# Shifting two operand pairs by 64 bytes in SBUF: block sums against gate and up weights, turned probabilities against values

## The reference

```
def swiglu(x, w_gate, w_up, w_down):
    return (jax.nn.silu(x @ w_gate) * (x @ w_up)) @ w_down
...
    for i in range(DEPTH):
        h = rms_norm(x, ffn1_norm[i])
        x = x + 0.5 * swiglu(h, ffn1_w_gate[i], ffn1_w_up[i], ffn1_w_down[i])
        ...  # the mixer: x = x + even_mixer(...) or odd_mixer(...)
        h = rms_norm(x, ffn2_norm[i])
        x = x + 0.5 * swiglu(h, ffn2_w_gate[i], ffn2_w_up[i], ffn2_w_down[i])
```

## Time and profile before

| | us |
|---|---|
| three runs | 1920.60, 1921.14 (median), 1924.37 |
| the profiled execution, first to last instruction | 1922.5 |
| PE busy in it | 1887.3 |
| DVE busy | 1462.5 |
| ACT busy | 1020.9 |
| POOL busy | 193.0 |

### The profile page before, as it was taken

How to read it: one execution, slowest core, us unless ns; L and a number is a source line. 1 busy time by engine, 2 the same in 40 slices (tenths; PEclk the granted TensorE clock), 3 DMA queues, 4 the chain that set the end, 5 groups by cost and what they waited for, 6 DMA issues and landing times.

```text
span 1922.5 us, 31441 instructions
## 1 busy us (share of the span) xinstructions
PE 1887.3 (98%) x11902; PEld 1674.8 (87%) x11902; DVE 1462.5 (76%) x2330; ACT 1020.9 (53%) x1640; POOL 193.0 (10%) x251
## 2 busy tenths in 40 slices
PE   7999999999999999999999999999999999999999
PEld 6899799888878899898889989887778779898997
DVE  8878487667779778597887949756988878687684
ACT  7546154477776455264644626454455766364451
POOL 1311010000001111010110101011111001011010
PEclk9999999999999999999999999999999999999999
DMA  7666862321126655462466646166765376566441
GB/s 240 169 171 182 131 188 61 110 77 57 65 102 173 170 151 152 149 175 97 136 167 165 166 132 181 50 152 161 171 148 133 85 202 171 157 168 168 133 115 66
DMA packets 94662, 271.18 MB, mean 141 GB/s; under 512 B 10568, under 2 KB 10824, under 8 KB 94512
## 3 DMA queue, kind: packets, MB, share of 16 engines
q1 hardware_dynamic: 63456, 201.22, 31.7%
q0 software_dynamic: 29232, 64.50, 19.4%
q10 hardware_dynamic: 1824, 3.44, 1.0%
HBM read 223.07 MB, written 2.28 MB: 117 GB/s over the span
## 4 chain that ended last, share of the span: by engine, by line
PE 85%; DVE 8%; ACT 3%; issue 2%; DMA 1%; ACTq 0%; DVEq 0%
PE ps_unit L797 12%; PE ps_unit L798 12%; PE ps_unit L799 12%; PE ps_y L861 6%; PE ps_y L863 6%; PE ps_y L862 6%; PE ps_s L861 4%; PE ps_s L863 4%; PE ps_s L862 4%; PE ps_t L861 4%; PE ps_t L863 3%; PE ps_t L862 3%; PE ps_s L797 1%; PE ps_s L798 1%; PE ps_s L799 1%
## 5 line engine op out<-in xcount | busy, mean ns | idle before, releaser
L1398 ACT ACTIVATE gw_hi<-gu 128x512 fp32r<-128x512 f32 (+1 forms) x400 | 318.9, 799 | 151.0 <-PE ps_s L863 67.5
L1932 DVE TENSOR_TENSOR gw_lo<-gu,gw_hi 128x512 fp32r<-128x512 f32 (+1 forms) x400 | 354.8, 901 | 49.0 <-ACT gw_hi L1398 36.7
L797 PE MATMUL ps_unit<-a_hi,w_hi 128*128 128x512 f32 x892 | 352.8, 395 | 9.2 <-DVE w_lo L1860 6.5
L798 PE MATMUL ps_unit<-a_lo,w_hi 128*128 128x512 f32 x892 | 349.1, 391 | 0.0
L799 PE MATMUL ps_unit<-a_hi,w_lo 128*128 128x512 f32 x845 | 330.1, 391 | 0.0
L1333 ACT ACTIVATE w_hi<-raw 128x1024 fp32r<-128x1024 f32 (+1 forms) x125 | 125.2, 1003 | 314.0 <-PE ps_unit L799 296.3
L797 PEld LDWEIGHTS ps_unit<-a_hi,w_hi 128*128 128x128 f32 x892 | 168.4, 189 | 48.8 <-DVE w_lo L1860 9.4
L2065 DVE TENSOR_TENSOR t<-ps_unit,half 128x512 f32<-128x512 f32 x96 | 66.4, 691 | 172.4 <-PE ps_unit L799 171.8
L798 PEld LDWEIGHTS ps_unit<-a_lo,w_hi 128*128 128x128 f32 x892 | 168.4, 189 | 33.2
L799 PEld LDWEIGHTS ps_unit<-a_hi,w_lo 128*128 128x128 f32 x845 | 159.5, 189 | 34.1
L861 PE MATMUL ps_y<-xu_hi,gw_hi 128*128 128x256 f32 x640 | 180.3, 282 | 0.3 <-ACT sqb L1402 0.3
(11 more groups left out here) (322 smaller groups left out, 4666.9 us busy)
## 6 DMA issues: line engine op xcount, KB each, us to landing
gu<-gu_stream_dram SPq DMA_DIRECT2D x176, 512.0 KB, 5.2
raw<-w_stream_dram SPq DMA_DIRECT2D x136, 512.0 KB, 3.3
gu<-gu_stream_dram SPq DMA_DIRECT2D x80, 256.0 KB, 3.0
gu<-gu_stream_dram POOLq DMA_DIRECT2D x80, 256.0 KB, 4.5
gu<-gu POOLq DMA_DIRECT2D x80, 256.0 KB, 3.3
w_lo<-raw POOLq DMA_DIRECT2D x28, 512.0 KB, 5.1
raw<-w_stream_dram SPq DMA_DIRECT2D x32, 384.0 KB, 3.5
w_lo_3rd<-raw POOLq DMA_DIRECT2D x15, 512.0 KB, 5.2
```

The costliest lines, as they stand in the source:

```text
L797: pe.matmul(ps, lhs_hi, rhs_hi, start=first, stop=False)
L798: pe.matmul(ps, lhs_hi, rhs_lo, start=False, stop=False)
L1398: act.activation(gw_hi[:, w, :], src, ACT.Copy).then_inc(gw_hi_done, 1)
L1932: dve.tensor_tensor(gw_lo[:, w, :], src, gw_hi[:, w, :].bitcast(F32), ALU.subtract).then_inc(gw_lo_done, 1)
```

## The change

Three gaps of 64 bytes are put into the layout. One moves xu_hi and xu_lo from 64 to 0 modulo 128 (gw stays at 64); one moves pt_hi and pt_lo in the same way (v stays at 64); the third moves what follows pt by another 64, so that all of these tiles have moved by 128 and keep their place modulo 128. No instruction is added, removed or moved on any engine; only addresses differ.

```
+
+HALF_LINE = 64
+
...
         gw_lo = sb("gw_lo", [P, 7, PIECE], F32R)
+        top[0] += HALF_LINE
         xu_hi = sb("xu_hi", [P, PAIRS, 3 * TH], F32R)
         xu_lo = sb("xu_lo", [P, PAIRS, 3 * TH], F32R)
...
         probs = sb("probs", [P, 2, T])
+        top[0] += HALF_LINE
         pt_hi = sb("pt_hi", [P, 14, P], F32R)
         pt_lo = sb("pt_lo", [P, 14, P], F32R)

+        top[0] += HALF_LINE
         shared = top[0]
```

## The result

The changed kernel takes 1929.41 us (median of five runs, 1927.55 to 1930.11) where the kernel before, run beside it, takes 1921.14 us (1920.54 to 1924.37). The ratio is 1.0036 with a 95% interval of 1.0026 to 1.0047: it is slower, by 5.0 to 9.0 us. The time lies above the predicted range.

What follows compares the result with a forecast made beforehand. The prediction took PE, busy 98% of the span, as the bound. Its terms -3.6 + 7.3 - 0.6 = +3.1 us on the median 1921.1 gave 1924.2 us, stated as 1923.5 us, range 1900 to 1927 us.

Steps and rivals of the forecast that it cites:

- PE sets the time, and its pace is what counts: Whole kernel: PE busy 98% of the span, so longer or shorter matmuls of the long streams are paid almost in full.
- "If xu takes the place of xs", group 1, -3.6 us: Four groups of 324 matmuls: xu also at 113.3 ns, 0.9 us less each, 3.6 us less in all.
- Groups 2 and 3, +7.3 us: Eight groups of 660 matmuls: all keep the slow 117.8 ns, 0.9 us more each, 7.3 us more in all.
- pt and v, -0.6 us: 192 pt matmuls of 256 columns: from 118 towards 113.3 ns, 0.6 us less taken, bounds 0 and 1.3 us less.
- The waits of PE, 0: Groups 2 and 3: one early and one late wait might let the pace become fast; nothing taken for either.
- the 0.7 us that the prediction took off for a freed group: Groups 2 and 3: a wait freeing one now and then takes about a microsecond off, 1924.2 to 1923.5 us.
- The prediction's 1.4 us between the profiled execution and the median: Whole kernel before: profiled execution put 1.4 us over the median of three runs, so the forecast counts from the median.
- the slower rival: Group 1: waits for DVE bring the slow pace, 0.5 us more each; 1930 us; chance 0.07, including a worse new place.
- The fast pace throughout: Groups 1 to 3: all at 113.3 ns, the slow pace kicked out or ending itself; -19.8 us, 1901 us; chance 0.28.
- The rule of the Trainium skill that the prediction weighed: PE: streamed operand and weights read through independent ports, so addresses would not matter; 1921 us; chance 0.06.

## Why the prediction was wrong, step by step

- **PE sets the time, and its pace is what counts.** Right. The difference lies in the 256-column streams, 6.1 us by their bounds. The waits in which the profiles also differ, at 204.95 us and the one of the earlier trace rows, are taken up above and below; neither follows the place of xu alone.
- **"If xu takes the place of xs", group 1, -3.6 us.** This is the step that failed. It took a place to be what the distance leaves modulo 128. By +64 xu came to a new place with a pace of its own, 117.8 ns instead of 113.3, and group 1 won 4 x 0.28 = 1.1 us: 2.5 us less than the term. The mechanism of the term was right for the place meant: at +192 group 1 is 36.73 us, 0.96 less than before. The prediction did have the doubt (+64 against -64 modulo 256), but used it as a condition of a rival and left it out of its own sum.
- **Groups 2 and 3, +7.3 us.** Right: 8 x 0.90 = 7.2 us. The kick that xu gave was gone and the slow pace lasted for all 660 matmuls. It came about by another way than the one assumed: xu does not share the slow pace of xs, it runs at 117.8 ns in group 1 too, beside a fast xs. That the two paces are the same number is luck for this term. At +192 the way is the assumed one: xu runs at 117.8 ns in groups 2 and 3 and at 113.3 in group 1.
- **pt and v, -0.6 us.** Nothing; the kernel with this part alone is at 0.9998 (0.9989 to 1.0007). In the changed kernel nine pt matmuls of 256 columns take 439.42 - 438.36 = 1.06 us, 118 ns each, as six did before:

```profile
438.36 0.28 PE L803 MATMUL ps_y<-pt_hi,v_hi 128*128 128x256 f32 x1
...
439.42 0.22 PE L803 MATMUL ps_y<-pt_hi,v_hi 128*128 128x128 f32 x1
```

- **The waits of PE, 0.** Right for the profile of after, where the wait of the earlier trace rows is missing and no group was freed or lost by it. Elsewhere it is longer than before's 0.25 us: 1.72 us with xu moved by 64, 1.42 by 128, 2.12 by 192, and 0.51 in the second profile of before. These are microseconds that the sum has no term for; what sets their length stays open.
- **What carries it out of the range.** With the step that failed set right, and the 0.6 us of pt taken out, the sum becomes 1921.1 + 7.2 - 1.1 = 1927.2 us, at the end of the stated range; the 0.7 us that the prediction took off for a freed group had no counterpart. The measured median is 2.2 us higher. The baseline may hold most of that: the five runs of before beside the changed kernel have a median of 1921.1 us, the larger sets 1922.0 to 1922.8 us, and 1922.7 + 7.2 - 1.1 = 1928.8 us. That is argued and not shown, and the wait above is another candidate. (The prediction's 1.4 us between the profiled execution and the median compares a span with a device time; like with like it is 1924.37 - 1921.14 = 3.2 us. The sum does not use it.)
- **The rivals.** The time came out close to that of the slower rival, 1930 us, but its mechanism did not take place: in the changed kernel PE has no wait in group 1 of the first block, with DVE busy for 36.15 of 38.20 us there (the windows: PE, PEld, DVE, ACT, POOL):

```profile
38.00:76.20 38.20, 38.20 (x324) 37.21 (x323) 36.15 (x53) 25.87 (x45) 6.19 (x7) 1.00 0.77 206
```

- The fast pace throughout did not come, since xu at +64 does not kick. It is there to be had: xu at +192 with one extra matmul ahead of each group 2 and 3 gives 1905 us, where that rival said 1901. The rule of the Trainium skill that the prediction weighed (page "TensorE: Matmul & The Clock Gate", section "Step-by-step: what each phase is for", two independent read ports) would, read as the prediction read it, have left the kernels that differ in addresses alone equal. The runs disagree with that reading: addresses alone give 113.3, 117.8, 119 or 120 ns for xu beside gw, and 1922.5 to 1929.4 us in all.

In one sentence: xu at 119.0 ns was dear for its 288 matmuls in a group 2 or 3, but it put the 372 matmuls with xs at 114.4 ns; moved, xu saves 288 x 1.05 ns = 0.3 us and xs loses 372 x 3.2 ns = 1.2 us (means over all starts of one group: xu 119.01 to 117.96 ns, xs 114.43 to 117.64 ns).

## What to carry to other kernels

Where the profile shows one shape of matmul at two paces, try several distances between the two operands before a rule behind them is believed, and modulo more than one power of two: here, two paces at two places could not tell a period of 128 bytes from one of 256. Look at what a slow piece does to the piece behind it before it is made faster: the slower operand was the one that kept the other one fast. Where a long stream enters at the slow pace, a single cheap matmul of another place or width at its head can be tried; here, with xu moved by 192, it is worth 0.9% of the whole kernel against before.

## What the runs showed of the hardware that was not expected

- Pace of a 256-column float32r matmul beside the same gw, by the distance of the two operands modulo 256: 0: 120 ns, once eight or so have run; +64: 117.8; 128: about 119, with single starts 115 to 123 ns apart; -64: 113.3 or 117.8, by what PE ran before. At 512 columns it was 226.7 ns at 0 and 233.5 at -64, in different products.
- The two paces at -64 are stable: 660 matmuls at either one. Down units (512 columns at 0) leave the slow one behind, the plain tiles (512 columns at -64) the fast one. One matmul of 256 or of 64 columns at 0, or one of 512 at -64, selects the fast one; one of 256 at -64 does not (seven groups of eight). At 128, twelve matmuls of xu in a row leave the fast one behind, 24 the slow one and 36 the fast one. So neither the place nor the width of what ran before decides alone.
- Behind a late start of PE either pace can follow. Behind the same wait of 1.2 to 1.3 us one group came back to the fast pace (64 columns) and one lost it (the changed kernel with the extra matmul), and of the twelve late pieces of before eight changed their pace from one execution to the other.
- What inside PE does this stays open. One idea is that the extra matmul shifts the reads of the moving operand against those of the weight loads, and that a wait does so by chance; it is argued and not shown. The records do not show such a shift: at either pace nearly every weight load is recorded to start 2 to 5 ns behind the matmul in front of it.
- The fastest kernel here, xu moved by 192 and one extra matmul ahead of each group 2 and 3, takes 1905.13 us, 0.9911 (0.9896 to 0.9926) of the kernel before.
